# High weights times high and low rows as one 512-wide product in the MLP up projections

## What is computed

```python
h2 = _rms_norm(x, g_pre_mlp[l])
m = jnp.square(jax.nn.relu(h2 @ w_up[l])) @ w_down[l]          # w_up 1024 x 4096
...
def swiglu(h, w_in, w_out):                                     # w_in 1024 x 5632, twice
    gate, up = jnp.split(h @ w_in, [D_FF_2], axis=-1)
    return (jax.nn.silu(gate) * up) @ w_out
```

## Time and profile before

| | |
|---|---|
| median of 3 runs | 1042.73 us (1042.41 to 1044.97) |
| the profiled execution's own time | 1042.56 us |
| its span in the trace | 1040.8 us |
| granted TensorE clock, mean | 0.996 |
| busy share: TensorE, VectorE, ScalarE, GpSimd | 96%, 61%, 47%, 7% |
| matmuls | 6300 |
| chain that ended last | TensorE 82%, VectorE 10%, ScalarE 4% |

### The profile page before, as it was taken

How to read it: one execution, slowest core, us unless ns; L and a number is a source line. 1 busy time by engine, 2 the same in 40 slices (tenths; PEclk the granted TensorE clock), 3 DMA queues, 4 the chain that set the end, 5 groups by cost and what they waited for, 6 DMA issues and landing times.

```text
span 1040.8 us, 14909 instructions
## 1 busy us (share of the span) xinstructions
PE 998.4 (96%) x6300; PEld 895.8 (86%) x6300; DVE 638.2 (61%) x659; ACT 489.0 (47%) x549; POOL 74.5 (7%) x87
## 2 busy tenths in 40 slices
PE   5999999989999999999989999999989999999997
PEld 5887777879999987998878999999879889999995
DVE  5555775666655556668865655455569966555553
ACT  4665446255643435642223634344358845434341
POOL 0100000000000001006530000000003100000000
PEclk9999999999999999999999999999999999999999
DMA  8555332437554542853303554544434537454531
GB/s 303 201 197 203 122 122 102 162 121 286 200 183 182 202 162 81 302 184 122 122 1 121 223 205 165 210 175 178 144 139 183 195 139 276 181 202 162 206 118 40
DMA packets 27138, 177.51 MB, mean 171 GB/s; under 512 B 3392, under 2 KB 3648, under 8 KB 7360
## 3 DMA queue, kind: packets, MB, share of 16 engines
q1 hardware_dynamic: 27072, 176.55, 46.0%
HBM read 175.49 MB, written 1.05 MB: 170 GB/s over the span
## 4 chain that ended last, share of the span: by engine, by line
PE 82%; DVE 10%; ACT 4%; issue 2%; DMA 1%; POOL 1%; DVEq 0%; POOLq 0%; ACTq 0%; SPq 0%
PE ps L1373 25%; PE ps L1375 25%; PE ps L1374 25%; DVE wL L857 4%; PE ps L1702 3%; PE ps L1405 2%; ACT wH L467 1%; ACT xn L471 1%; DVE FF L1303 1%; DVE FF L1279 1%; DVE RR L869 0%; POOL st L394 0%; DVE xr L1057 0%; DMA raw<-w_stream 0%; DVE xn L883 0%
## 5 line engine op out<-in xcount | busy, mean ns | idle before, releaser
L857 DVE TENSOR_TENSOR wL<-raw,wH 128x2048 fp32r<-128x2048 f32 (+3 forms) x164 | 368.6, 2257 | 219.6 <-ACT wH L467 219.5
L467 ACT ACTIVATE wH<-raw 128x2048 fp32r<-128x2048 f32 (+3 forms) x164 | 304.0, 1862 | 179.6 <-PE ps L1375 160.0
L1373 PE MATMUL ps<-aL,wH 128*128 128x256 f32 x1088 | 308.1, 283 | 0.8 <-DVE wL L857 0.8
L1375 PE MATMUL ps<-aH,wH 128*128 128x256 f32 x1088 | 307.9, 283 | 0.0
L1374 PE MATMUL ps<-aH,wL 128*128 128x256 f32 x1088 | 307.9, 283 | 0.0
L1373 PEld LDWEIGHTS ps<-aL,wH 128*128 128x128 f32 x1088 | 208.7, 192 | 2.1 <-issue 0.9
L1374 PEld LDWEIGHTS ps<-aH,wL 128*128 128x128 f32 x1088 | 208.7, 192 | 1.2
L1375 PEld LDWEIGHTS ps<-aH,wH 128*128 128x128 f32 x1088 | 208.7, 192 | 0.0
L1373 PE MATMUL ps<-wL,RR 128*128 128x512 f32 (+1 forms) x384 | 149.9, 390 | 0.4 <-DVE RR L869 0.3
L1374 PE MATMUL ps<-wH,RR 128*128 128x512 f32 (+1 forms) x384 | 149.1, 388 | 0.0
L1375 PE MATMUL ps<-wH,RR 128*128 128x512 f32 (+1 forms) x384 | 148.8, 388 | 0.0
(11 more groups left out here) (183 smaller groups left out, 822.5 us busy)
## 6 DMA issues: line engine op xcount, KB each, us to landing
raw<-w_stream SPq DMA_DIRECT2D x153, 1024.0 KB, 4.8
bc<-rows_in SPq DMA_DIRECT2D x5, 512.0 KB, 7.2
raw<-w_stream SPq DMA_DIRECT2D x5, 512.0 KB, 3.6
FF<-rows_in SPq DMA_DIRECT2D x5, 512.0 KB, 7.1
raw<-w_stream SPq DMA_DIRECT2D x4, 576.0 KB, 4.4
raw<-w_stream SPq DMA_DIRECT2D x2, 768.0 KB, 7.7
xr<-x_in SPq DMA_DIRECT2D x2, 512.0 KB, 5.5
xn<-rows_in SPq DMA_DIRECT2D x1, 1024.0 KB, 4.6
```

The source lines that it names most:

```text
L467: e.activation(wH[:, i % NHL, 0:wd], raw[:, i % NRAW, 0:wd], ACT.Copy).then_inc(hi, 1)
L857: e.tensor_tensor(wL[:, i % NHL, 0:wd], raw[:, i % NRAW, 0:wd], h.bitcast(F32), ALU.subtract).then_inc(lo, 1)
L1373: e.matmul(out, lhs[0], rhs[1], start=start, stop=False)
L1375: return e.matmul(out, lhs[0], rhs[0], start=False, stop=stop)
```

## The change

Each step along the width of the 54 up chunks now has two matmuls in place of three. The high half of the weights is loaded once, and the moving operand is both halves of the rows side by side, 2 x 256 columns. The result fills a whole bank: its left half is high times high, its right half high weights times low rows. The low half of the weights times the high rows is added to the left half. For that `aH` and `aL` become the two parts of one buffer `aHL`. VectorE then adds the two halves of each bank by a reduction over two elements (`tensor_reduce` on `both_halves`), which writes 128x512 sums to SBUF. A chunk takes two banks (4 and 5, or 6 and 7, in turn), and TensorE waits for the sum of the chunk two before it. The turned first units move from banks 4 and 5 to banks 0 and 1. The squared ReLU of the later units is now one VectorE instruction on the sum (maximum with 0, times itself) and ScalarE only copies its high half. The order of the splits between the units is rewritten in both programs, and `lower_bounds` is cut in four pieces behind units 4 to 7.

```diff
@@ buffers and helpers @@
-        aH = sb("aH", [128, 8, 256], F32R)
-        aL = sb("aL", [128, 8, 256], F32R)
+        aHL = sb("aHL", [128, 2, 8, 256], F32R)
+        aH, aL = aHL[:, 0], aHL[:, 1]
...
+        def wide_bank(n):
+            return 4 + 2 * (n % 2)
+
+        def both_halves(b):
+
+            return ps[:, b:b + 2, :].rearrange("p b (h t) -> p b t h", h=2)
@@ ScalarE, squared-ReLU MLP @@
             for j in range(16):
...
-                e.activation(r, ps[:, up_bank(j), :].rearrange("p (f t) -> p f t", f=2), ACT.Relu).then_inc(relued, 1)
-                e.wait_ge(relued, j + 1)
+                if j > 2:
+                    split(31 + 2 * j)
+                e.wait_ge(hid_in, j + 1)
                 if j >= 4:
                     e.wait_ge(used, d_at("w_down", j - 4) + 1)
-                e.activation(hid[j % 4][0], r, ACT.Square).then_inc(hid_hi, 1)
+                e.activation(hid[j % 4][0], q, ACT.Copy).then_inc(hid_hi, 1)
@@ VectorE, squared-ReLU MLP @@
+                    if j > 2:
+                        split(31 + 2 * j)
+                    b = wide_bank(j)
+                    e.wait_ge(used, pair_at("w_up", 2 * j, 2 * j + 1) + 1)
+                    e.tensor_reduce(pre[j % 2], both_halves(b), AX, ALU.add).then_inc(summed, 1)
+                    e.wait_ge(summed, SUMMED["relu", j])
+                    e.scalar_tensor_tensor(q, pre[j % 2], 0.0, pre[j % 2], ALU.max, ALU.mult).then_inc(hid_in, 1)
+                e.wait_ge(hid_in, j + 1)
                 e.wait_ge(hid_hi, HID["relu", j])
                 low_half(hid[j % 4][1], q, hid[j % 4][0]).then_inc(hid_lo, 1)
@@ VectorE, SwiGLU MLPs @@
+                        add_halves(j, 2 * j)
+                        split(glu_lead(layer, j) + 5)
+                        add_halves(j, 2 * j + 1)
+                        e.wait_ge(summed, SUMMED[name, 2 * j + 1])
                     e.wait_ge(glu_sig, n)
-                    e.tensor_tensor(s, ps[:, b:b + 2, 0:256], s, ALU.mult).then_inc(glu_mul, 1)
+                    e.tensor_tensor(s, gate, s, ALU.mult).then_inc(glu_mul, 1)
                     e.wait_ge(glu_mul, 2 * n - 1)
-                    e.tensor_tensor(q, ps[:, b:b + 2, 256:512], s, ALU.mult).then_inc(glu_mul, 1)
+                    e.tensor_tensor(q, up, s, ALU.mult).then_inc(glu_mul, 1)
+                    if j:
+                        split(glu_lead(layer, j) + 6)
                     e.wait_ge(hid_hi, HID[name, j])
                     low_half(hid[j % 4][1], q, hid[j % 4][0]).then_inc(hid_lo, 1)
-                    split(plan[j])
+                    if j < 10:
+                        split(glu_lead(layer, j + 1) + 4)
@@ TensorE @@
+            def wide_part(i, banks):
+
+                h, l = weights(i)
+                for n, b in enumerate(banks):
+                    for k in range(8):
+                        c = slice((8 * n + k) * 128, (8 * n + k + 1) * 128)
+                        e.matmul(halves(b), h[:, c], aHL[:, :, k, :], start=k == 0, stop=False)
+                        last = e.matmul(ps[:, b, 0:256], l[:, c], aH[:, k, :], start=False, stop=k == 7)
+                last.then_inc(used, 1)
...
-                    if n < 4:
-                        e.wait_ge(copied, COPY["pre_mlp", n - 2])
-                    else:
-                        e.wait_ge(relued, n - 3)
-                    s_part(pair_at("w_up", 2 * n, 2 * n + 1), act, two(up_bank(n)))
+                    if n == 3:
+                        e.wait_ge(copied, COPY["pre_mlp", 1])
+                    elif n > 3:
+                        e.wait_ge(summed, SUMMED["relu", n - 2])
+                    wide_part(pair_at("w_up", 2 * n, 2 * n + 1), (wide_bank(n), wide_bank(n) + 1))
```

More of the change, by code:

```diff
@@ L157, in program, with glu_lead @@
     GLU = numbered(*[(s, j) for s, n in MLPS[1:] for j in range(n)])
+    SUMMED = numbered(*[("relu", j) for j in range(2, 16)], *[(s, f) for s, n in MLPS[1:] for f in range(2, 2 * n)])
+    def glu_lead(layer, j):
+        return at["s", ((f"ffn_in{layer}", 2 * j), (f"ffn_in{layer}", 22 + 2 * j)), 8]
     ctx = ExitStack()
@@ L273, in program @@
         htmp = [FF[:, j * 1024:j * 1024 + 1024].rearrange("p (a f t) -> p a f t", a=2, f=2) for j in range(2)]
+        pre = [FF[:, 2048 + 512 * j:2560 + 512 * j].rearrange("p (f t) -> p f t", f=2) for j in range(2)]
+        glu = [FF[:, 2048 + 1024 * j:3072 + 1024 * j].rearrange("p (f a t) -> p f a t", f=2, a=2) for j in range(2)]
         Q = FF[:, 0:2048].rearrange("p (h t) -> p h t", h=8)
@@ new lines, in lower_bounds @@
+                lam = cols[:, C_LAM:C_LAM + 8]
+                if piece == 0:
+                    linked(e.tensor_tensor(mx, l0, l1, ALU.max))
+                    settle()
+                    e.tensor_tensor(e0, l0, mx, ALU.subtract).then_inc(bound_dve, 1)
+                    e.tensor_tensor(e1, l1, mx, ALU.subtract).then_inc(bound_dve, 1)
+                elif piece == 1:
+                    e.wait_ge(bound_act, 1)
+                    linked(e.tensor_tensor(mx, e0, e1, ALU.add))
+                    settle()
+                    linked(e.reciprocal(mx, mx))
+                    settle()
+                    linked(e.tensor_tensor(lb, e0, mx, ALU.mult))
+                    linked(e.tensor_tensor(om, e1, mx, ALU.mult))
+                    e.scalar_tensor_tensor(nl, lam, -1.0, lam, ALU.mult, ALU.min).then_inc(bound_dve, 1)
+                elif piece == 2:
+                    e.wait_ge(bound_act, 2)
+                    e.tensor_scalar(w1, z, 1.0, None, ALU.add).then_inc(bound_dve, 1)
+                else:
+                    e.wait_ge(bound_act, 3)
+                    linked(e.tensor_scalar(w1, w1, 1.0, 1e-30, ALU.subtract, ALU.max))
+                    linked(e.tensor_scalar(nl, lam, -1.0, 0.0, ALU.mult, ALU.max))
+                    settle()
+                    linked(e.reciprocal(c4, w1))
+                    settle()
+                    linked(e.tensor_tensor(c4, c4, z, ALU.mult))
+                    settle()
+                    linked(e.tensor_tensor(c4, c4, lw, ALU.mult))
+                    linked(e.tensor_scalar(w1, w1, 1e-30, None, ALU.is_le))
+                    settle()
+                    linked(e.tensor_tensor(w1, w1, z, ALU.mult))
+                    settle()
+                    linked(e.tensor_tensor(c4, c4, w1, ALU.add))
+                    settle()
+                    linked(e.tensor_tensor(c4, c4, nl, ALU.add))
+                    settle()
+                    e.tensor_scalar(c4, c4, 4.0, None, ALU.mult).then_inc(bound_dve, 1)
+                    e.wait_ge(bound_dve, 5)
+                    e.tensor_scalar(c8, c4, -2.0, None, ALU.mult).then_inc(bound_dve, 1)
@@ L1125, in _ @@
                 r, q = htmp[j % 2][:, 0], htmp[j % 2][:, 1]
[L1126 to L1128 removed]
+                if j < 2:
+                    e.wait_ge(relued, j + 1)
+                    e.tensor_tensor(q, r, r, ALU.mult).then_inc(hid_in, 1)
+                else:
+                    if j > 2:
[6 more added lines that the diff above has]
+                e.wait_ge(hid_in, j + 1)
                 e.wait_ge(hid_hi, HID["relu", j])
                 low_half(hid[j % 4][1], q, hid[j % 4][0]).then_inc(hid_lo, 1)
[L1131 removed]
+                if j == 2:
                     split(37)
[L1133 to L1137 removed]
+                elif 4 <= j < 8:
+                    lower_bounds(j - 4)
             split(62)
```

128 lines of the change are left out of this document (45 added, 83 removed).

## The result

The changed kernel takes **1038.01 us** (median of 4 runs, 1036.66 to 1038.66) against 1043.85 (4 runs, 1042.41 to 1045.47) before: a ratio of 0.9942, with a 95% interval of 0.9921 to 0.9963. It is faster by about 6 us, where I had forecast 11.5, and 1038.0 lies above the range of 1028.5 to 1037.0. The profiled execution took 1037.73 us.

The account below looks back on a forecast made before the run. The prediction took TensorE's matmuls to bound the kernel: 864 fewer at 13.3 ns save 11.5 us, so 1042.56 becomes 1031.1, plus 0.17 for the median, 1031.2 us; range 1028.5 to 1037.0.

Parts of the forecast that it names:

- What bounds the kernel: All three MLPs: TensorE is busy throughout at full clock, so only its instructions' number and length set the time.
- The fixed 13.3 ns of a matmul: TensorE: each matmul pays some 13.3 ns on top of its columns; 864 fewer matmuls gain 11.5 us.
- Now: 227 + 120 = 347 ns: Up chunks: a step's wide and narrow matmul together take 347 ns, where three narrow ones took 360 ns.
- rival A: Up chunks: the two-piece moving operand takes an extra start, pair up to 360 ns, up to 1042.7 us; chance 0.07.
- VectorE's sums: VectorE: 54 new reductions of 1.22 us each, 66 us in all, hidden beside TensorE.
- Rivals B: VectorE: short rows slow each sum to 2.6 us, losing 9.2 of the 11.5 us, 1040.4 us; chance 0.05.
- C: VectorE: each reduction row costs its own start, sum 6.5 us, VectorE becomes the bound, 1225 us; chance 0.04.
- The beginning of the first MLP: First MLP, tightest place: chunk 39's low half ends at 266.6, needed at 270.2; slack 3.6 us, no cost.
- Rival D: First MLP's beginning stalls by 2 to 4 us from late loads or pieces, 1033 to 1035 us; chance 0.06.
- The last units of the SwiGLU MLPs: Last three units: chain 10.2 us in an 11.1 us period; last low half at 6.7 us, needed at 8.2; no cost.
- The low-clock stretches: Between stages: two stretches at 1.2 GHz, each costing about 2 us; timing moves could lose or add one.
- The range: Whole kernel: 1028.5 to 1037.0 us, covering clock stretches, rounding, sums up to 2.0 us and stalls at the first MLP's beginning.

Follow-up runs that it names:

- e4: Changed kernel with the low weights also multiplied by both halves of the rows, so all up-chunk matmuls are 512 wide; 1125.06 us (one run).
- e7: Changed kernel with the wide product taken apart again into three 256-wide matmuls per step, sums and waits kept; 1042.91 us, ratio 0.9998 against before.
- e11: The kernel of e6 timed again, 16 wide then 16 narrow matmuls per chunk; 1031.48 us, ratio 0.9888 against before.
- e1: Changed kernel with the two row halves side by side per block, so the wide moving operand is one piece; 1037.48 us, ratio 0.9951 against before.
- e2: Changed kernel with eight wide matmuls, then eight narrow ones, in each output instead of in turn; 1033.17 us, ratio 0.9909 against before.
- e8: The kernel of e2 with each of VectorE's 54 sums done twice; 1041.89 us (one run), 8.7 above e2.
- e3: Changed kernel with the narrow product added to the right half of the bank instead of the left; 1038.08 us (one run).
- e5: Changed kernel with two wide matmuls, then two narrow ones, and so on in each output; 1031.61 us (one run).
- e9: Changed kernel with lone narrow matmuls between pairs of wide ones (wide, wide, narrow three times, two wide, five narrow); 1034.2 us (one run).
- e13: Changed kernel with runs of three wide, three narrow, three and three, two and two per output; 1032.46 us (one run).
- e10: Changed kernel with lone wide matmuls between pairs of narrow ones (five wide; narrow, narrow, wide three times; two narrow); 1035.34 us (one run).
- e6: Changed kernel with all 16 wide matmuls of a chunk first, then its 16 narrow ones; 1032.35 us (one run).

## Why the prediction was right or wrong

**What bounds the kernel: right.** TensorE is busy for the whole of every MLP after the change too, and all of the time moved as its matmuls did.

**The fixed 13.3 ns of a matmul: right, as a cost between matmuls of one width.** e4 has 226.9 ns at 512 columns in two pieces, e7 a chunk of 48 matmuls in 5.76 us (120 ns each), and with nearly all changes of width removed (e11) a pair costs 12.5 to 13.0 ns less than three narrow ones. By the 2.5 ns of the Trainium skill ("TensorE: Matmul & The Clock Gate", section on the 56 ns gap), 2.2 us would have been saved, an estimate; no run here supports it for these matmuls.

**The step that failed: "Now: 227 + 120 = 347 ns".** Both terms came from rows in which every matmul stands behind one of its own width, and the pair changes width at each instruction. It measured 352.8 ns. That takes 864 x 5.8 = 5.0 us from the 11.5, 12 down chunks take 0.4 more, and the 6 us that were measured are the rest. I had asked whether the operand's two pieces cost something (rival A), which the chip answered with nothing (e1, e4), and had not asked whether the mixture did. The trace before held a hint: in the earlier trace rows ten 512-wide matmuls behind one another take 227 ns, but a down chunk of 24 with the up chunk's 256-wide ones ahead of it took 5.47 us, where 24 x 227 ns are 5.45, so that a change of width had a price there too, some 27 ns over the five matmuls behind it; the same mixture, one by one, stood nowhere.

**Rival A: wrong in its mechanism, half right in its size.** It had the pair at up to 360 ns because of the pieces. The pair lay midway between 347 and 360, for another reason, and the chance of 0.07 for a smaller share was too low: a price taken as zero between bounds of 0 and 13.3 ns should have kept more than that.

**VectorE's sums: right.** "I take 1.22 us" measured 1221 to 1224 ns, so that rows of two elements, 1 KB apart, from PSUM cost what long rows from SBUF cost. Rivals B (2.6 us) and C (6.5 us) are excluded. All 54 are hidden: e7 gives a ratio of 0.9998.

**The beginning of the first MLP: right, nearly to the step.** The chain worked out had the split behind which chunk 36 stands end at 249.4 and chunk 39's low half at 266.6. VectorE after:

```profile
247.60 2.29 DVE L872 TENSOR_TENSOR wL<-raw,wH 128x2048 fp32r<-128x2048 f32 x1 [1.05 <-ACT wH L482]
249.81 1.22 DVE L1152 TENSOR_REDUCE FF<-ps 128x512 f32<-128x1024 f32 x1
...
264.65 4.49 DVE L872 TENSOR_TENSOR wL<-raw,wH 128x2048 fp32r<-128x2048 f32 x2 [2.21 <-ACT wH L482]
```

The first split ends at 249.9, the first of the double row at about 266.9; the chunk was needed at 271.1, the pace being slower than forecast. Rival D did not happen, nor at the faster pace of e2 and e11.

**The last units of the SwiGLU MLPs: right.** Forecast: the last low half 6.7 us behind the last up chunk, needed at 8.2. That chunk ended at 729.21; VectorE after:

```profile
729.41 1.23 DVE L1265 TENSOR_REDUCE FF<-ps 128x512 f32<-128x1024 f32 x1 [1.35 <-PE ps L1441]
731.40 0.69 DVE L1280 TENSOR_TENSOR FF<-FF 128x512 f32<-128x512 f32 x1 [0.77 <-ACT FF L751]
...
733.14 2.29 DVE L872 TENSOR_TENSOR wL<-raw,wH 128x2048 fp32r<-128x2048 f32 x1 [0.32 <-ACT wH L482]
735.35 0.68 DVE L884 TENSOR_TENSOR RR<-FF,RR 128x512 fp32r<-128x512 f32 x1
```

It ends at 736.03, 6.8 us behind, and TensorE has no wait. That the slack is of this size and no more, e8 showed: 2.4 us more for the two sums of the unit and more behind them, and TensorE waits 2.3 us there.

**The low-clock stretches: right in size, not in what makes them come and go.** They do not follow the change; they differ between executions. Over the two stretches between stages, the changed kernel and e11 (the clock is the third number from the end):

```profile
397.00:412.00 15.00, 12.55 (x52) 9.63 (x51) 9.85 (x10) 6.54 (x11) 3.24 (x5) 0.89 0.38 141
535.00:552.00 17.00, 14.35 (x63) 11.54 (x63) 9.81 (x11) 4.99 (x6) 2.21 (x3) 0.90 0.18 63
```

```profile
397.00:412.00 15.00, 11.64 (x52) 8.65 (x51) 9.62 (x10) 7.28 (x9) 3.23 (x5) 1.00 0.37 141
535.00:552.00 17.00, 14.62 (x71) 12.00 (x72) 11.03 (x12) 5.00 (x6) 1.88 (x3) 1.00 0.19 63
```

Where the second is absent, its stage is 1.6 us shorter (11.1 against 12.7 us between two marks, in e1, e3, e5, e9, e11 and e13); in four of these (e1, e3, e9, e11) the stage before was 1.4 us longer, so that nothing came of it, and in e10 that stage was longer and the second stretch stayed. One execution's total says nothing about 1.6 us, which is why e5 and e6 were compared by their chunks.

**The range.** It had held all that I knew to be unknown (clock, length of the sum, stalls), and the step that failed was in none of its terms, because it had been taken as read.

## What to carry to other kernels

Take a matmul's price from neighbours such as it will have, the five ahead of it and not only the last one: a duration between instructions of one shape isn't the price in a mixture, and a trace that lacks the mixture leaves an unknown to be bounded from both sides. When narrow products are merged into a wide one and a narrow one is left over, issue the wide ones of a chunk first and the narrow ones behind them; here that nearly doubled the gain of the change (11.4 us against about 6) by the order of the loops alone. And work out the slack of the engine that takes over the work at the thin places by hand: here its steps came within 0.5 us, though with twice the sums (e8) the first MLP lost 2.1 us and not 0 to 1.

## What was unexpected of the hardware

- A change of matmul width costs time: 352.8 ns for a 512-wide and a 256-wide matmul in turn, against 226.8 + 120.0 = 346.8 in runs. The loss is in the start behind the wide one (236.0 ns against 226.8), while the start behind the narrow one comes 3 ns sooner (116.8). Behind a long run of narrow matmuls it is spread over five wide ones, 27 ns in all (e2, and 5.47 against 5.44 us for a down chunk, before and e4). Regular twos lose 3 ns per cycle of four, twos and threes mixed 7 per cycle; I have no mechanism that gives all of these.
- A moving operand in two pieces of 256 columns, 8 KB apart, runs at the rate of one piece (226.9 ns, e4), and matmuls one behind the other into the same cells of PSUM cost nothing.
- The same wait of 2.3 us in e8 was followed by a stretch at the lower clock in the third MLP (0.76 on average over 7 us) and by none in the second (1.00).
- VectorE's sum over rows of two elements from PSUM takes 1.22 us for 1024 elements, as a sum over rows of 128 in SBUF does.
